# A second raw buffer for the modulation weights, and another order of loads, in a one-core transformer layer

## The reference

```python
c_act = silu(c)
mod = (c_act @ w_ada + b_ada).reshape(B, 3, 3, 1024)     # nine vectors of 1024
h = modulate(rms_norm(x, g1), mod[0, 0], mod[0, 1])
x = x + 0.5 * mod[0, 2] * swiglu(h, ffn1_w_in, ffn1_w_out)        # D_FF = 2816
h = modulate(rms_norm(x, gmix), mod[1, 0], mod[1, 1])
proj = h @ w_mix_in                                      # 512 pool, 512 u, 512 v columns
ya = pool_mixer(proj[..., :512]); yb = u * spatial_gating(v)      # v: gelu, layer norm, w_spatial
x = x + mod[1, 2] * (concat([ya, yb]) @ w_mix_out)
h = modulate(rms_norm(x, g2), mod[2, 0], mod[2, 1])
x = x + 0.5 * mod[2, 2] * swiglu(h, ffn2_w_in, ffn2_w_out)
y = rms_norm(x, g_final)
```

## Time and profile before

| | |
|---|---|
| median of 3 runs | 903.28 us (903.22 to 905.3) |
| profiled execution | 902.2 us, span 900.5 us |
| TensorE busy | 851.4 us, 95% |
| VectorE busy | 642.0 us, 71% |
| ScalarE busy | 379.8 us, 42% |
| transfers | 142.02 MB, mean 158 GB/s |
| mean granted clock of TensorE | 0.977 of full |

### The profile page before, as it was taken

How to read it: one execution, slowest core, us unless ns; L and a number is a source line. 1 busy time by engine, 2 the same in 40 slices (tenths; PEclk the granted TensorE clock), 3 DMA queues, 4 the chain that set the end, 5 groups by cost and what they waited for, 6 DMA issues and landing times.

```text
span 900.5 us, 14159 instructions
## 1 busy us (share of the span) xinstructions
PE 851.4 (95%) x5767; PEld 758.6 (84%) x5767; DVE 642.0 (71%) x919; ACT 379.8 (42%) x528; POOL 43.7 (5%) x56
## 2 busy tenths in 40 slices
PE   4899866999999999999999999999999999999997
PEld 3677755988899999878787898899988899999886
DVE  4577845787688887877755869988875488886443
ACT  6232313521366664124423337566531265665233
POOL 0000000000001000000121000001000000010000
PEclk9899977999999999999999999999999999999998
DMA  9969246767565665841834523475574556664322
GB/s 276 286 192 261 65 139 158 203 198 220 137 173 148 165 179 169 274 132 47 261 90 141 140 75 84 104 184 153 163 237 128 140 132 174 175 142 108 97 65 93
DMA packets 214781, 142.02 MB, mean 158 GB/s; under 512 B 6216, under 2 KB 193724, under 8 KB 214716
## 3 DMA queue, kind: packets, MB, share of 16 engines
q1 hardware_dynamic: 209764, 132.19, 50.9%
q0 software_dynamic: 4896, 8.92, 6.3%
q10 hardware_dynamic: 56, 0.01, 0.0%
HBM read 130.08 MB, written 2.10 MB: 147 GB/s over the span
## 4 chain that ended last, share of the span: by engine, by line
PE 70%; DVE 13%; DMA 7%; ACT 4%; issue 3%; SPq 3%; POOL 0%; DVEq 0%; ACTq 0%
PE ps L1835 12%; PE ps L1831 12%; PE ps L1833 12%; PE ps L1658 11%; PE ps L1659 11%; PE ps L1660 11%; DVE work L1120 3%; DMA w_raw<-in_ffn_w_in_dram 2%; DMA ada_raw<-in_w_ada_dram 1%; DMA sw_raw<-in_ffn_w_out_dram 1%; DVE h_lo L1067 1%; DMA ada_first<-in_w_ada_dram 1%; ACT sw_hi L816 1%; DMA ws_raw<-in_w_spatial_dram 1%; ACT w_split L655 1%
## 5 line engine op out<-in xcount | busy, mean ns | idle before, releaser
L1831 PE MATMUL ps<-sums_hi,sw_hi 128*128 128x256 f32 x544 | 152.2, 280 | 1.8 <-ACT ev L823 1.8
L1833 PE MATMUL ps<-sums_lo,sw_hi 128*128 128x256 f32 x544 | 152.8, 281 | 0.0
L1658 PE MATMUL ps<-b_hi,sw_hi 128*128 128x512 f32 (+1 forms) x374 | 143.6, 384 | 2.1 <-DVE sw_lo_b L1275 2.1
L1659 PE MATMUL ps<-b_lo,sw_hi 128*128 128x512 f32 (+1 forms) x374 | 141.4, 378 | 0.0
L791 ACT CAST sw_hi<-sw_raw 128x1024 fp32r<-128x1024 f32 (+2 forms) x102 | 119.8, 1180 | 34.5 <-DVE sw_raw L1240 22.0
L1831 PE MATMUL ps<-h_hi,sw_hi 128*128 128x256 f32 x408 | 114.3, 280 | 8.3 <-DVE sw_lo_a L1253 8.3
L1835 PE MATMUL ps<-sums_hi,sw_lo_a 128*128 128x256 f32 x408 | 115.7, 284 | 0.0
L1833 PE MATMUL ps<-h_lo,sw_hi 128*128 128x256 f32 x408 | 114.6, 281 | 0.0
L1658 PE MATMUL ps<-h_hi,w_split 128*128 128x512 f32 (+1 forms) x240 | 95.9, 400 | 17.6 <-DVE w_split L1015 12.1
L1253 DVE TENSOR_TENSOR sw_lo_a<-sw_raw,sw_hi 128x1024 fp32r<-128x1024 f32 x68 | 98.9, 1455 | 9.1 <-ACT sw_hi L791 6.8
L1831 PEld LDWEIGHTS ps<-sums_hi,sw_hi 128*128 128x128 f32 x544 | 102.9, 189 | 2.3 <-issue 1.7
(11 more groups left out here) (191 smaller groups left out, 1595.6 us busy)
## 6 DMA issues: line engine op xcount, KB each, us to landing
sw_raw<-in_ffn_w_in_dram SPq DMA_DIRECT2D x170, 256.0 KB, 4.2
sw_raw<-in_w_ada_dram SPq DMA_DIRECT2D x16, 1024.0 KB, 6.1
ada_raw<-in_w_ada_dram SPq DMA_DIRECT2D x24, 512.0 KB, 4.8
sw_raw<-in_ffn_w_out_dram SPq DMA_DIRECT2D x32, 384.0 KB, 4.6
sw_raw<-in_ffn_w_out_dram SPq DMA_DIRECT2D x32, 320.0 KB, 3.6
w_raw<-in_ffn_w_in_dram SPq DMA_DIRECT2D x19, 512.0 KB, 6.9
sw_raw<-sw_raw POOLq DMA_DIRECT2D x34, 256.0 KB, 3.4
ada_first<-in_w_ada_dram SPq DMA_DIRECT2D x14, 512.0 KB, 7.3
```

Of the source, the lines that this page charges most:

```text
L1658: nc.tensor.matmul(dst, w_h, a_h, start=start, stop=False)
L1659: nc.tensor.matmul(dst, w_h, a_l, start=False, stop=False)
L1831: nc.tensor.matmul(dst, w_h[:, k, :], src_hi[:, k, :], start=start and k == 0, stop=False, skip_group_check=True)
L1833: nc.tensor.matmul(dst, w_h[:, k, :], src_lo[:, k, :], start=False, stop=False, skip_group_check=True)
```

## The change

It makes five edits. (1) Parts 0 to 8 are now all read in the plain steps, in turn through `ada_raw` and a second buffer `more_raw`; each buffer has its own semaphores. Which part goes where, when it is loaded and in which plain step it is read changes. Part 8 is no longer hosted, and the hosted parts 9 to 19 each move up one down step. `more_raw` lies where `ada_last` was, so SP waits before its first load for the eighth block of first rows. (2) The two v blocks are loaded one down step later and two steps later. (3) Block 0 of v is split during down step 5, ahead of that step's update. (4) The pairs 0 and 1 of the mix projection no longer wait for the splits of the v blocks; pair 1 waits for the landing of v block 1 instead, and all that stands behind them in SP's list, the spatial weights too, is issued sooner. (5) Pair 2 of the mix projection is loaded ahead of part 21.

```diff
-    ADA_PLAIN = {0: (0,), 1: (1, 2), 2: (3,), 4: (4, 5), 5: (6, 7)}
-    ADA_MIX = tuple(range(20, 24))
-    ADA_RAW = tuple(range(8)) + ADA_MIX
-    HOSTED = ({down_item(0, g, m): 8 + 6 * g + m for g in range(2) for m in range(6)},
+    ADA_PLAIN = {0: (0,), 1: (1, 2), 2: (3,), 3: (4,), 4: (5, 6), 5: (7, 8)}
+    ADA_IN = ((0, 2, 4, 6, 7, 20, 21, 22, 23), (1, 3, 5, 8))
+    HOSTED = ({down_item(0, g, m): 9 + 6 * g + m for g in range(2) for m in range(6 - g)},
...
+            before_more = sb("before_more", [P, 8 * KA * TH + 2 * GF * T], F32, over_a)
+            more_raw = sb("more_raw", [P, 2, KA // 2, UNIT], F32, over_a)
...
-    def load_two(w, col, s, chunk):
-                raw_free(chunk)
+                if chunk > MIXIN + 3:
+                    raw_free(chunk)
+                elif s:
+                    sp.wait_ge(raw_full[1], (MIXIN + 1) // 2 * 32 + 32)
...
     def load_ada(part):
-                n = ADA_RAW.index(part)
+                b = int(part in ADA_IN[1])
+                n = ADA_IN[b].index(part)
                 for s in range(2):
                     if n:
-                        sp.wait_ge(ada_link, used(ADA_RAW[n - 1], (s + 1) * KA // 2))
+                        sp.wait_ge(ada_link, used(ADA_IN[b][n - 1], (s + 1) * KA // 2))
...
             for j in range(2, PLAIN[0]):
                 load_pair(ffn1_w_in, j, j % 2, UP1 + j)
-                for part in {2: (0,), 3: (1, 2), 4: (3,), 5: (4,), 6: (5, 6), 7: (7,)}.get(j, ()):
+                if j == 3:
+                    sp.wait_ge(first_rows, KD)
+                for part in {2: (0,), 3: (1,), 4: (2,), 5: (3, 4), 6: (5,), 7: (6, 8, 7)}.get(j, ()):
                     load_ada(part)
...
                 load_down2(0, 1, m)
-                if m == KD - 4:
+                if m in (KD - 3, KD - 2):
                     sp.wait_ge(sw_used[0], pieces(0, up_item(0, NS[0] - 1) + 1))
-                    for kq in range(2):
-                        load_v(w_mix_in, kq)
+                    load_v(w_mix_in, m - (KD - 3))
...
-            load_ada(21)
             for q in range(2, 4):
                 load_two(w_mix_in, q * UNIT // 2, q % 2, MIXIN + 2 + q)
+                if q == 2:
+                    load_ada(21)
...
+                if m == KD - 3:
+                    split_hi(MIXIN)
                 square(m, 0)
-            split_hi(MIXIN)
...
+                if m == KD - 3:
+                    split_lo(MIXIN)
                 update_last(0, m)
                 add_squares(X_AT[0] + m + 1)
-
-            split_lo(MIXIN)
```

More of the change, by code:

```diff
@@ L119, in added @@
         return 16 * sum(1 for j in range(i % 2, i + 1, 2) if j in UP_ITEMS[f])
-    ADA_PLAIN = {0: (0,), 1: (1, 2), 2: (3,), 4: (4, 5), 5: (6, 7)}
-    ADA_MIX = tuple(range(20, 24))
-    ADA_RAW = tuple(range(8)) + ADA_MIX
-    HOSTED = ({down_item(0, g, m): 8 + 6 * g + m for g in range(2) for m in range(6)},
+    ADA_PLAIN = {0: (0,), 1: (1, 2), 2: (3,), 3: (4,), 4: (5, 6), 5: (7, 8)}
+    ADA_IN = ((0, 2, 4, 6, 7, 20, 21, 22, 23), (1, 3, 5, 8))
+    HOSTED = ({down_item(0, g, m): 9 + 6 * g + m for g in range(2) for m in range(6 - g)},
               {down_item(1, 0, m): 24 + m for m in range(4)})
     TAKES = ((0, 2), (2, 8), (8, 12), (12, 13), (13, 14))
-    assert sorted(ADA_RAW + tuple(HOSTED[0].values()) + tuple(HOSTED[1].values())) == list(range(2 * UNITS))
+    assert sorted(ADA_IN[0] + ADA_IN[1] + tuple(HOSTED[0].values()) + tuple(HOSTED[1].values())) == list(range(2 * UNITS))
     def used(part, steps=KD // 2):
@@ L220, in build_program @@
         with ExitStack() as over_a:
+            before_more = sb("before_more", [P, 8 * KA * TH + 2 * GF * T], F32, over_a)
+            more_raw = sb("more_raw", [P, 2, KA // 2, UNIT], F32, over_a)
+        with ExitStack() as over_a:
             before_xs = sb("before_xs", [P, 8 * KA * TH + GF * T + (GF - KD) * T], F32, over_a)
@@ L261, in build_program @@
         first_full = [sem(f"first_full{k}") for k in range(KD)]
-        ada_full = [sem("ada_full0"), sem("ada_full1")]
+        ada_full = [[sem(f"ada_full{b}{s}") for s in range(2)] for b in range(2)]
         mix_full = sem("mix_full")
@@ L449, in load_ada @@
             def load_ada(part):
-                n = ADA_RAW.index(part)
+                b = int(part in ADA_IN[1])
+                n = ADA_IN[b].index(part)
                 for s in range(2):
                     if n:
-                        sp.wait_ge(ada_link, used(ADA_RAW[n - 1], (s + 1) * KA // 2))
+                        sp.wait_ge(ada_link, used(ADA_IN[b][n - 1], (s + 1) * KA // 2))
                     k0 = part % 2 * KA + s * KA // 2
-                    sp.dma_start(ada_raw[:, s], w_ada_v[:, k0:k0 + KA // 2, ada_cols(part)])\
-                      .then_inc(ada_full[s], 16)
+                    sp.dma_start((ada_raw, more_raw)[b][:, s], w_ada_v[:, k0:k0 + KA // 2, ada_cols(part)])\
+                      .then_inc(ada_full[b][s], 16)
             def load_first(k):
@@ L1130, in ada_own @@
             def ada_own(part):
-                count = 16 * (ADA_RAW.index(part) + 1)
-                ada_steps(part, lambda q: ada_raw[:, q // 2, q % 2, :], lambda q: (ada_full[q // 2], count))
+                b = int(part in ADA_IN[1])
+                count, raw = 16 * (ADA_IN[b].index(part) + 1), (ada_raw, more_raw)[b]
+                ada_steps(part, lambda q: raw[:, q // 2, q % 2, :], lambda q: (ada_full[b][q // 2], count))
             def ada_hosted(f, i):
```

## The result

The changed kernel took 875.83 us (median, 874.34 to 876.57) against 903.25 us for the kernel before in the same runs: a ratio of 0.970, 95% interval 0.9674 to 0.9725. The profiled executions have spans of 874.8 and 900.5 us.

What follows compares the result with a forecast made beforehand. It took TensorE, busy 95% of the span, to be held by late weight splits from the single raw buffer's reload loop. Terms 20.5 - 0.8 + 3.2 + 3.8 = 26.7 us gave 875.5 to 876.6, stated as 876.2 us; range 872.5 to 887.

Steps and rivals of the forecast that it cites:

- The plain steps: Plain steps to third block: 20.5 us of VectorE's waits for parts and late pairs go; third block starts at 132.8.
- The splits of chunks 6 and 7: VectorE in the plain steps: they end at 100.9 and 111.6, just in time, so 0 us of TensorE waits.
- The cover of part 8: VectorE after part 7: its 2.8 us for part 8 are covered by a 3.81 us wait for the first block.
- The term of 0.8 us: Start of the blocked steps: third block may start at the low clock, costing 0.8 us, ends 0 and 2.4.
- second rival: Start of the blocked steps: clock stays low, 1.6 us more than taken, and again after, 878 to 880; chance 0.15.
- The end of the first feed-forward: Down steps: later v loads and an early split of v block 0 save 3.2 us, ends 1.5 and 3.7.
- The room that I gave VectorE: Down step 5: the early split takes part 19's place (4.5 us), and a down step is 7.5 us of TensorE.
- The spatial weights: Transposes of the spatial weights: loaded 20 us sooner, the 1.9 us wait goes; 3.8 us in all, ends 1.9 and 4.0.
- the clock behind the transposes: After the spatial weights' transposes: without the stand the low clock of 0.66 goes, 1.7 us.
- Late loads: Plain steps, first rival: loads are late all the same, 8.3 us of waits return, 885 us; chance 0.16.
- the 4 us that I had put on it: Plain steps: pair 4 would land some 4 us later behind part 1, still before its use.
- The slow side: Down step 5: a late v block 0 holds ScalarE's casts and TensorE's down steps, making the kernel slower; chance 0.03.

Runs made afterwards that it cites:

- e4_v: Edits 2 and 3 alone on the kernel before, part 19 still in down step 5: ratio 0.9995 (0.9979 to 1.0012) to the kernel before.
- e6_vload: Edit 2 alone on the kernel before, v block 0 split at its old place: 899.26 us, ratio 0.9965.
- e5_ws: Edits 4 and 5 alone on the kernel before: 900.76 us, ratio 0.9978.
- e3_order: The changed kernel with its two buffers, but parts put ahead of the pairs in the queue again: 876.64 us, ratio 0.9724.
- e12_nows: The changed kernel without edits 4 and 5: 877.0 us beside 876.02 for the changed kernel in the same set.
- e9_after: The changed kernel run again, unchanged, as yardstick of a later set: 876.02 us.
- e1_plain: Edit 1 alone on the kernel before: 883.1 us, ratio 0.9798.
- e10_fill2: The same kernel as e7_fill in another set: 875.14 us beside 876.02 for the changed kernel.
- e7_fill: The changed kernel with 30 unused matmuls more in the stand before the third block: 876.33 us against 875.83 for the changed kernel in another set.
- e8_chain: The changed kernel with part 7 through the second buffer and part 8 hosted again in the down steps: 873.69 us, ratio 0.9671.
- e11_three: The changed kernel with part 7 in the second buffer and part 8 in a third one: 869.46 us, beside 876.02 for the changed kernel.

## Why the prediction was right, step by step

**The plain steps.** The sum took 20.5 us from VectorE's waits and the third block at 132.8; it started at 132.44, stage A is 20.67 us shorter. Part 7 was read by 114.71 where 115.2 stood. The step that carried it, removing the waits of rows 5 and 6 but for 0.64 us, was right: 0.7 us are left. That the stage agrees within 0.2 us is in part luck, since its old form varies: it took 96.56, 96.84, 97.61 and 99.09 us in the four profiles that have it (before, e4_v, e6_vload, e5_ws), the new form 75.8 to 76.3 in the five without filler. Between the means it is 21.5 us. The splits of chunks 6 and 7 were put at 100.9 and 111.6, and ended at 97.84 + 2.28 = 100.1 and 108.61 + 2.28 = 110.9. TensorE waited for neither. The cover of part 8, 3.81 us, shrank to 1.06 as worked out. The mechanism as told was too narrow in one point: I had the pairs leave sooner and the parts double-buffered as two halves of one cure. e3_order shows that the second is enough, with the parts read in the new steps.

**The clock.** The term of 0.8 us was mis-sized for the profiled execution: B grew by 2.50, the upper end I had named (2.4), and that is the second rival's state, though none of the four times reached that rival's 878 to 880. Over executions it is 0 to 2.5 (e12_nows 0.0, e9_after 1.5, e1_plain and e3_order 2.45), so a value between was a fair guess for the median. By the rule of the Trainium skill ("TensorE: Matmul & The Clock Gate", section "HAM oscillation — how this bites in real kernels") bursts shorter than the waits between them start cold. The third block's start at 0.50 in the profile after, behind a burst of 3.0 us and a stand of 3.9, agrees; e12_nows, where the fall lay over the first two blocks and cost nothing, shows that the rule gives no price by itself.

**The end of the first feed-forward.** 3.2 us stood in the sum, D gave 3.72, of which 2.35 for the loads and 1.37 for the early split (by e6_vload). The room that I gave VectorE was there only because part 19 moves; the prediction did say so, and e4_v shows what it is worth: all of it.

**The spatial weights.** 3.8 us in the sum, 3.58 in the two profiles (E 1.95, F 1.63). But the second half, the clock behind the transposes, is the step that does not hold in general. Stands of 0.9 to 1.7 us at the same place (e1_plain 1.5, e4_v 1.7, e6_vload 0.9, e12_nows 1.4) left F at 124.4 in those four profiles. I read one execution's low stretch as a fixed cost. For the median the term is about 1.9 us (e5_ws, 0.1 to 3.8) or less (e12_nows, 1.0), and the sum of terms then is 25 rather than 27. The median difference was 27.4 us here and 26.5 in the later set, with intervals of 24.8 to 29.4 and 24.5 to 28.2 us that both hold 25; the plain steps, 1 us dearer in the mean of the old profiles than in the one that was read, would bring 25 to 26.

So the mechanism was right in its main parts, and the hit on the median, 876.2 against 875.83, is closer than the terms deserve: the profiled pair is 25.7 us apart, 1.0 less than the sum, with the clock mis-sized by 1.7 us and the other terms 0.7 us in the other direction.

**The rivals.** Late loads: no split waited for a pair, and VectorE's waits for parts are 0.2 us. One count in the argument against this rival was short: five of the waits came after 104, four for parts and one for a cast. In e3_order pair 4 left right behind part 2, 4.8 us after the start of plain step 2 against 1.0 in the profile after, and TensorE still didn't wait. By the Trainium skill ("DMA: Bandwidth & Descriptors", section "Queues, rings and completion order") a transfer's semaphore lands only after all earlier writes of each DMA engine, so a part issued just ahead delays a pair. The traces agree and show how much: the two loads of pair 4, from issue to landing in the median, after and e3_order:

```profile
w_raw<-in_ffn_w_in_dram SPq DMA_DIRECT2D x2, 512.0 KB, 4.5
w_raw<-in_ffn_w_in_dram SPq DMA_DIRECT2D x2, 512.0 KB, 6.8
```

Pair 7 shows the same two values. A part just ahead costs a pair 2.3 us of landing, less than the 4 us that I had put on it, and this kernel has the room for it. The slow side (a late v block in front of ScalarE's work) had no trace: the cast at step 5 did not wait.

## What to carry to other kernels

Where a queue is served in order and a single buffer's reload stands in it, add up the waits of the engine that consumes the buffer: that sum, less what other causes keep, was the gain to within 0.2 us in this pair of profiles, and to within 1 us of the mean. A second buffer and a better order in the queue cured the same wait here; try the one that costs less, and don't count both. An early piece of work is free only in a step with room, so move what fills the step first (e4_v against the changed kernel), and a low clock seen behind one short stand should be priced as a chance, not as a sum.

## What was unexpected in the hardware

The plain steps ran at two paces. From the start of step 2 to the last of its 288 products it was 67.04 us in the profiles after, e1_plain, e3_order and e10_fill2, and 65.78 us in e7_fill, e8_chain, e9_after, e11_three and e12_nows: 0.2336 and 0.2292 us from one 128x512 matmul to the next, both at a granted clock of 1.00, and both for the same kernel (after and e9_after). Nothing in the views says why. The 11.0 us a step of the prediction are the fast pace. In the changed kernel the pace does not reach the span, because the chain to the third block ends later; it only moves the stand before the first block, 1.5 us in the profile after and 3.3 in e9_after. In e8_chain, whose first block follows the plain steps without a stand, the slow pace would cost up to 1.3 us; that is an estimate from the two lengths, as its one profile had the fast pace.
